# First block's attention stage: the copies of turned probabilities go to ScalarE, one row maximum goes ahead of the index scores, the top-k rounds stand in four steps running

## What is computed

```python
def hybrid_layer(x, ...):
    h = rmsnorm(x, g_pre_mix)
    proj = h @ w_in                       # 256 x 3404, split into the inputs of four kinds of attention
    o_a = dsa_attention(...)              # A: index scores, top 64 keys of each row, then softmax over those
    o_b = forgetting_attention(...)       # B: softmax with a decay
    o_c = differential_attention(...)     # C: difference of two softmaxes, normed
    o_d = sliding_window_sink_attention(...)  # D: window of 128, with a sink
    mix = concatenate(o_a, o_b, o_c, o_d)
    x = x + rmsnorm(mix @ w_out, g_post_mix)
    ...                                   # MLP and a gated projection
```

## Time and profile before

| | us |
|---|---|
| median of 3 runs | 2182.11 |
| lowest, highest | 2181.06, 2182.19 |
| the profiled execution | 2180.04 |
| its span from first to last instruction | 2178.2 |

### The profile page before, as it was taken

One profiled execution on the slowest core, in us unless ns is written; L12 is line 12 of the kernel. 1 busy time (PEld: TensorE's weight loads), 2 busy tenths in 40 slices (PEclk: granted clock), 3 DMA queues, 4 the chain that ended last, 5 costly groups with the idle time before them and its releaser, 6 DMA issues.

```text
span 2178.2 us, 26315 instructions
## 1 busy us (share of the span) xinstructions
PE 2043.5 (94%) x9270; PEld 1672.1 (77%) x9270; DVE 1193.5 (55%) x1360; ACT 873.9 (40%) x997; POOL 62.1 (3%) x88
## 2 busy tenths in 40 slices
PE   4998999899899998999999989997999999998997
PEld 3886888687778877877877778886877887787885
DVE  3675555557555555433766564445532757555455
ACT  3544444456253444311345434443321335443442
POOL 2210000022000000000000000000000000000000
PEclk9987999999799999956999999998965999999998
DMA  5413555452245544643655645554644555654553
GB/s 192 148 52 121 177 189 173 156 168 90 77 155 180 192 150 157 207 87 108 209 177 174 208 145 169 179 183 165 205 113 126 173 175 174 193 187 132 177 180 115
DMA packets 214819, 345.17 MB, mean 158 GB/s; under 512 B 13355, under 2 KB 82219, under 8 KB 214721
## 3 DMA queue, kind: packets, MB, share of 16 engines
q1 hardware_dynamic: 213440, 342.10, 49.4%
q0 software_dynamic: 384, 1.31, 0.2%
q10 hardware_dynamic: 897, 0.49, 0.1%
HBM read 342.74 MB, written 1.12 MB: 158 GB/s over the span
## 4 chain that ended last, share of the span: by engine, by line
PE 86%; DVE 5%; issue 3%; DVEq 3%; ACT 2%; POOL 0%; POOLq 0%; ACTq 0%
PE G L573 21%; PE G L574 21%; PE G L579 20%; PE T L598 5%; PE A L573 3%; PE A L574 3%; PE A L579 3%; PE G L720 3%; PE G L723 2%; PE A L641 2%; DVE wlo L1386 1%; ACT arena L1007 1%; PE A L646 1%; DVEq L1431 1%; ACT whi L1007 1%
## 5 line engine op out<-in xcount | busy, mean ns | idle before, releaser
L1386 DVE TENSOR_TENSOR wlo<-raw,whi 128x2048 fp32r<-128x2048 f32 (+3 forms) x320 | 676.5, 2116 | 661.3 <-ACT whi L1007 661.1
L1007 ACT ACTIVATE whi<-raw 128x2048 fp32r<-128x2048 f32 (+3 forms) x320 | 565.9, 1769 | 789.0 <-PE G L579 718.5
L573 PE MATMUL G<-whi,XH 128*128 128x512 f32 x1696 | 680.1, 401 | 6.6 <-DVE XL L1401 6.6
L574 PE MATMUL G<-whi,XL 128*128 128x512 f32 x1696 | 669.7, 395 | 0.0
L579 PE MATMUL G<-wlo,XH 128*128 128x512 f32 x1696 | 419.3, 389 | 0.0
L573 PEld LDWEIGHTS G<-whi,XH 128*128 128x128 f32 x1696 | 325.0, 192 | 77.0 <-issue 6.4
L574 PEld LDWEIGHTS G<-whi,XL 128*128 128x128 f32 x1696 | 324.6, 191 | 68.1 <-issue 1.9
L579 PEld LDWEIGHTS G<-wlo,XH 128*128 128x128 f32 x1696 | 318.2, 188 | 66.9 <-DVE wlo L1386 0.7
L598 PE MATMUL T<-ident,arena 128*128 128x128 f32 x812 | 136.8, 313 | 25.9 <-ACT arena L1007 19.3
L598 PEld LDWEIGHTS T<-ident,arena 128*128 128x128 f32 x812 | 109.0, 161 | 44.4 <-ACT arena L1007 18.5
L1007 ACT ACTIVATE arena<-G,nm 128x128 f32<-128x128 f32 (+2 forms) x104 | 50.3, 493 | 196.0 <-DVE nm L1427 151.2
(11 more groups left out here) (187 smaller groups left out, 1882.2 us busy)
## 6 DMA issues: line engine op xcount, KB each, us to landing
raw<-in_w_in SPq DMA_DIRECT2D x112, 1024.0 KB, 7.0
raw<-in_w_mlp_up SPq DMA_DIRECT2D x32, 1024.0 KB, 5.4
raw<-in_w_mlp_down SPq DMA_DIRECT2D x32, 1024.0 KB, 5.0
raw<-in_w_ffn_gate SPq DMA_DIRECT2D x44, 512.0 KB, 4.1
raw<-in_w_ffn_up SPq DMA_DIRECT2D x44, 512.0 KB, 5.0
raw<-in_w_ffn_down SPq DMA_DIRECT2D x44, 512.0 KB, 3.3
raw<-in_w_out SPq DMA_DIRECT2D x16, 1024.0 KB, 5.0
raw<-in_w_ret_proj SPq DMA_DIRECT2D x16, 1024.0 KB, 5.1
```

What stands on the lines that cost most here:

```text
L573: nc.tensor.matmul(dst(m), hx[:, k0 + k, rows], hi[:, k, :], start=first and k == 0, stop=False)
L574: nc.tensor.matmul(dst(m), lx[:, k0 + k, rows], hi[:, k, :], start=False, stop=False)
L1007: return nc.scalar.activation(out_, in_, func, **kw)
L1386: tt(wlo[:, c % PARTS, 0:n], raw[:, slot, 0:n], whi[:, c % PARTS, 0:n].bitcast(F32), ALU.subtract).then_inc(s_lo.sem, 1)
```

## The change

VectorE takes the maximum of job 0 first, and `scores(1)` follows in the `beside` of step 0, ahead of the `lo` part. The two top-k rounds of steps 0, 1, 4, 5 stand in steps 1, 2, 3, 4, and the mask in step 4. The turned tiles of the first block's jobs are copied by ScalarE: after the exponentials of job q (and, in step 2, after turn C's copies and the projection) come the copies of job q-1, and behind the last step those of job 9. `RL` moves to the place of `PT`, so the first of these copies waits for the end of `scores(1)`.

```diff
-        RL = room(12952, IDX_HEADS, S)
+        RL = room(15000, IDX_HEADS, S)
@@ ScalarE
+            def job_copies(L, q):
+                for kt in range(JOBS1[q][1] + 1):
+                    t = T_JOB + job_banks(JOBS1, q) + kt
+                    act.wait_ge(s_t.sem, s_t.at(0, L, t + 1))
+                    act_(PT[:, q % 2, kt, :], T[:, t % 2, :], ACT.Copy).then_inc(s_tfree.sem, 1)
@@ ScalarE, the loop over the jobs
                     if q == Q_TURN_C + 1:
                         turn_copy(0, L, T_JOB + job_banks(JOBS1, Q_TURN_C) - 2, 4, QT[:, 13:17])
                         project(0, 6, LAST1)
-                    elif q == Q_TURN_D:
+                    if q == 1:
+                        act.wait_ge(s_rlf.sem, s_rlf.at(0, L, 2))
+                    if q:
+                        job_copies(L, q - 1)
+                    if q == Q_TURN_D:
                         turn_copy(0, L, T_JOB + job_banks(JOBS1, Q_TURN_D) - 2, 4, QT[:, 17:21])
-                    elif q in (3, 4):
+                    if q in (3, 4):
                         hi(0, L, 0, 11 + q)
+                job_copies(L, len(JOBS1) - 1)
@@ VectorE, run_jobs
-                    if 1 <= q <= len(jobs):
+                    if jobs is JOBS2 and 1 <= q <= len(jobs):
                         copy_turned(blk, L, q - 1, jobs, t0, dst)
@@ VectorE, first block
-                scores(1)
                 def beside(q):
                     if q == 0:
+                        scores(1)
                         lo(0, L, 0, 13)
                     elif q == 3:
                         dve.wait_ge(s_evac.sem, s_evac.at(0, L, CH1))
                         rope(dve, nc.vector, RT, D_Q, 4, HD, 0).then_inc(s_rope.sem, 1)
-                    if q in (0, 1, 4, 5):
+                    if q in (1, 2, 3, 4):
                         pick(1, TOPK // 4)
-                    if q == 5:
+                    if q == 4:
                         mask(1)
```

## The result

The changed kernel took 2183.15 us, the median of 20 runs (2179.90 to 2188.32), beside 2180.93 for the kernel before (20 runs, 2175.83 to 2182.69). The ratio is 1.0014, with a 95% interval of 1.0008 to 1.0020: slower by 3.1 us, between 1.7 and 4.4. (The two medians differ by 2.2 us; differences in this text go by the ratio.) The forecast was slower by 7.6. The measured time lies within the range and the sign is as forecast, but the size is 3.1 and not 7.6. That is less than the 0.2% which the prediction took for the least that a measurement can tell; with 20 runs of each kernel the interval still leaves out "no difference".

A forecast was written before the change was run, and what follows sets the result against it. TensorE was taken to bound the kernel, with this stage a chain of latencies. 2 x 3.8 = 7.6 us on the profiled 2180.04 gives 2187.6; the median, 2.1 above, is 2189.7 us, range 2175 to 2197.

The forecast's parts named there:

- early walk: First layer, job 0 up to the second turn held by copies: engine order followed step by step, lateness growing to 4.9 us.
- job 0's gain: Start of the stage: maximum 2.4 us earlier, exponentials 1.9; worth 0.5 us at its turn, and unused.
- turn C: TensorE's turn needing job 0's copied tile: starts at 124.3, not 123.36, late by 0.9 us.
- division of job 0: VectorE, without job 1's copy, waits 5.3 us for job 0's outputs, 125.9 to 131.2; the division brings it to 131.9.
- maxima of jobs 3, 4 and 5: VectorE, behind the moved rounds: job 3 at 134.0 against 131.57, job 4 at 139.9 against 136.44, job 5 at 144.9.
- turn D: TensorE waits for ScalarE's copies of job 4, behind job 5's exponentials: 148.4 against 143.46, late by 4.9 us.
- turn of the mix: End of the stage: last division at 182.1, 4.2 us late, or 3.4 like against like; 3.8 a layer taken.
- the clock behind the middle of the stage: TensorE's granted clock: half from 143.3 to 160.4 and again from about 170 to the dense matmuls behind the stage.
- its sign of being wrong: Prediction wrong if job 4's copies let TensorE's next turn come before 146, or clock is full where half was put.
- no second fall: Rival: clock stays full from 160 to the end, change worth about nothing, 2182; chance 0.18 with other small net.
- job 1: VectorE does scores and `lo` first, so this maximum comes at 121.4, not 120.52; the turn needing job 0's copy 0.9 late.
- The rule on queues: ScalarE's and VectorE's queues: a ready tile cannot pass the exponentials; otherwise the two held-up turns start about 1.2 and 3.5 us earlier.

The follow-up runs named there:

- the version without the late maxima: Kernel before with copies on ScalarE and four rounds and the mask in VectorE's wait of step 2: 2164.49 us with copies ahead of the exponentials, 2171.17 us behind.
- the run of the rounds with VectorE's copies: Kernel before with four top-k rounds and the mask ahead of the division of job 0, copies still by VectorE: 2181.08 us, ratio 1.0006.
- the best version: Kernel before with ScalarE's copies ahead of the exponentials from step 3 on, last four rounds and mask in VectorE's wait of step 2: 2164.49 us, ratio 0.9923.

## Why the prediction was right in sign and wrong in size

**What held.** The early walk is right in mechanism and order: job 0's gain goes unused, turn C is late, VectorE stands idle before the division of job 0, the maxima of jobs 3, 4 and 5 come late, and turn D waits for ScalarE's copies. The sizes are another matter. This is how late each place is against the kernel before, on the stage's clock, in us:

| | forecast | first layer | second layer |
|---|---|---|---|
| turn C | 0.9 | 2.7 | 2.7 |
| division of job 0 | 0.6 | 4.0 | 5.0 |
| maximum of job 4 | 3.5 | 6.6 | 7.7 |
| turn D | 4.9 | 8.2 | 9.2 |
| maximum of job 9 | 3.8 | 6.5 | 7.5 |
| turn of the mix | 3.8 | 3.3 | 4.4 |
| first output unit behind the stage | 3.8 | 1.2 | 3.6 |

**The step that failed: the clock behind the middle of the stage.** The forecast put half clock "from 143.3 to 160.4 and again from about 170 to the dense matmuls", and carried 3.8 us a layer from the turn of the mix to the end of the kernel. Measured, half clock runs from 140 to 164 and then not again in the first layer; in the second it comes back at 583.6 only, behind the turn of the mix. Before, it had come at 167 and at 570, shortly after the maximum of job 9. From that maximum to the turn of the mix the kernel before takes 12.1 us and the one after 9.0 in both layers; the turns of eight that take 1.97 us before take 1.15 and 1.09 here. From the turn of the mix to the output unit it is 8.5 and 9.5 us before, 6.4 and 8.7 after. Together 9 us come back that the sum put at nothing. The prediction named this as its sign of being wrong, full clock where it put half, and its rival "no second fall" had the mechanism; the result lies between the two. That the missing fall is the cause is read from the traces; no run changed the clock by itself.

**The agreement at the turn of the mix is luck.** 3.3 and 4.4 us there are 7.7 together, against 7.6 forecast. They are the difference of two errors: turn D was later than forecast by 3.3 and 4.3 us, and most of that came back before the mix, where the clock stayed full.

**A term that was too small: "job 1".** `scores(1)` was put at 5.5 us, from the row in the old place. In the new place it took 113.61 to 120.48, 6.9 us, beside GpSimd's rotary embedding; the run without this work showed 3.83 for the part that took 5.70. This is most of why turn C is 2.7 us late and not 0.9. TensorE's wait before turn C, 3.35 us, was followed by the dip from 126.5 to 130, and the projection ran in it: from turn C to the turn of job 1 it takes 6.1 us, against 4.6 in the run without GpSimd's work, which has no dip there. By the division of job 0 the lateness is thus 4.0 us where 0.6 was forecast. Behind it the rounds and turn D add 4.2 us, and 4.3 were forecast: the excess at turn D in the first layer all comes from ahead of that division.

**How the parts share in it.** The forecast costed ScalarE's copies by their place behind the exponentials, at turn D, and gave the copies that VectorE is spared 1.8 us a layer. Measured, the copies are worth -7.6 us alone and -10.2 beside the two other parts (3.1 less 13.3), but only -1.9 beside the maximum and -3.3 beside the rounds. Each of these figures is uncertain by about 3 us. The maximum (+7.4) and the rounds (+3.1) cost time without the copies too. So the change is a gain of 8 to 10 us and a loss of 11 to 13, and a forecast of +7.6 in one sum showed neither.

**The rule on queues.** The Trainium skill, "TensorE: Matmul & The Clock Gate", in the section on the array of sub-arrays, calls the queues of ScalarE and VectorE strict first-in first-out. The trace agrees: in the kernel after, the two tiles of job 4 are turned by 147.39, but ScalarE copies them at 149.26, behind the exponentials of job 5:

```profile
149.26 1.09 ACT L1007 ACTIVATE arena<-T 128x512 f32<-128x512 f32 x2
```

What this costs is another matter. The copies ahead of the exponentials gave nothing in the changed kernel and 7 us in the version without the late maxima. Why it is so uneven is not settled: I take it that in the changed kernel the maxima, not the copies, set the pace, but no run shows this alone.

**What stays open.** The parts don't add up (-7.6, +7.4 and +3.1 make 2.9, and the three together measure 3.1, but the pairs differ from their sums by 3 to 6 us; the largest of these is clear of the intervals, the smallest isn't). The profiles show one execution each; the stages of one kernel differ between its two layers by up to 5.5 us (71.7 and 77.2 in the run of the rounds with VectorE's copies) where the order of work is the same and the granted clock differs:

```profile
110.00:190.00 80.00, 68.22 (x458) 59.47 (x457) 57.82 (x123) 33.01 (x101) 8.72 (x12) 0.87 0.18 58
510.00:595.00 85.00, 73.31 (x446) 64.79 (x446) 55.82 (x118) 32.68 (x101) 8.76 (x12) 0.80 0.16 59
```

What makes the clock fall in one layer and not in the other is open: in the best version it fell after a wait of 1.58 us in the second layer and not in the first. A step that is 1 us shorter on the path is worth more or less than 1 us by where it leaves the dips, and I have no way to foretell these from a trace.

## What to carry to other kernels

When side work (here top-k rounds) has to stand on the engine that also feeds the critical chain, put it where that engine waits, not where a step has room on paper: the same rounds cost 6 us more in front of three maxima than in the wait before the first division. Look in the written order for what the wait stands ahead of: with VectorE's copies the wait lay before a copy, the rounds placed behind that copy missed it, and the run gained nothing. Split a change of several parts before judging it: this one hides a gain of 7.6 us, and its best part with the rounds in the right place is 16.8 us faster. In a stage of short waits, follow the sum past the stage to the next dense matmuls: the same work from the turn of the mix to the output unit took 6.4 us at full clock and 8.5 to 9.5 with the clock down for a part of it, and this decided how much of the lateness remained.

## What was not expected of the hardware

Seven VectorE multiply-adds of 128x256 took 5.70 us beside four GpSimd tensor operations and 3.83 without them; in the trace of the changed kernel two of them carried the whole difference (1.49 and 1.34 us, the five others 0.48 to 0.49). These two are the ones that ran while GpSimd's last two operations did, until 116.96. One small negation behind a maximum took 0.41 us beside GpSimd's work in the kernel after, 0.50 in the one before, and 0.17 to 0.20 otherwise. Half clock for about 9 and 13 us more of a stage went with 3.7 and 5.5 us more of time, each in two layers of the same program.
